# Rewriting the two attention stages of a streaming encoder: masked queries for the streams' tile, quotients on GpSimd, the causal mask as a product, the output kept in SBUF

## The reference

```python
# layer 0, prompt: causal, with a cumulative log-forget bias per head
cum = transpose(cumsum(logf, axis=1))
s = einsum('bqhd,bkhd->bhqk', q, k) * scale + cum[..., :, None] - cum[..., None, :]
s = where(key_pos <= qpos, s, -1e30)
out = einsum('bhqk,bkhd->bqhd', softmax(s), v)
# layer 0, streams: the same over 128 cached and 16 new keys of the stream itself
# layer 1, prompt: own chunk of 64 and the 8 chunks before, bias by clipped distance
s = einsum('bqhd,bkhd->bhqk', q, k) * scale + rel_bias[head, clip(dist)]
# layer 1, streams: cached and new keys of the stream, the same bias
h = h + merge_heads(out) @ w_out
```

## Time and profile before

| | |
|---|---|
| median of 3 runs | 3518.08 us (3513.18 to 3521.7) |
| the profiled execution | span 3516.8 us, 1.3 us under the median |
| stretch from 400 to 856.5 us (fox) | PE busy 347.42 us, granted clock 0.90 |
| stretch from 2168 to 2543 us (band) | PE busy 293.32 us, granted clock 0.94 |

### The profile page before, as it was taken

The page is one execution under the profiler, slowest core; times in us unless marked ns, Lnnn a source line. Parts: engine busy times, 40 slices in busy tenths (PEclk is TensorE's granted clock), DMA queues, the critical chain, the costliest instruction groups (busy, mean ns, idle before and its releaser), DMA issues. The chain is left out here.

```text
span 3516.8 us, 47851 instructions
## 1 busy us (share of the span) xinstructions
PE 3217.5 (91%) x16000; PEld 2680.0 (76%) x16000; DVE 1489.9 (42%) x2930; ACT 1174.2 (33%) x2540; POOL 423.7 (12%) x686
## 2 busy tenths in 40 slices
PE   8999577776999999999989997888699999999998
PEld 7877366665878888888878886777677888888887
DVE  3121388887243333333332221776634333333333
ACT  4232266665142211112223323777623122111122
POOL 0000245542000000000000001444300000000000
PEclk9999799998999999999999998999999999999999
DMA  4885343452441111111014884444322111111111
GB/s 153 200 250 166 137 153 141 153 178 74 125 156 60 48 36 36 36 36 52 19 51 144 241 213 160 158 157 160 106 84 78 37 51 56 36 36 36 36 36 54
DMA packets 329715, 363.82 MB, mean 103 GB/s; under 512 B 25200, under 2 KB 270976, under 8 KB 323344
## 3 DMA queue, kind: packets, MB, share of 16 engines
q1 hardware_dynamic: 329616, 362.52, 32.8%
HBM read 255.23 MB, written 120.98 MB: 107 GB/s over the span
## 5 line engine op out<-in xcount | busy, mean ns | idle before, releaser
L251 PE MATMUL ffn_gu<-ffn_gh,ffn_xh 128*128 128x512 f32 x1584 | 635.2, 401 | 0.0
L253 PE MATMUL ffn_gu<-ffn_gh,ffn_xl 128*128 128x512 f32 x1584 | 619.6, 391 | 0.0
L252 PE MATMUL ffn_gu<-ffn_gl,ffn_xh 128*128 128x512 f32 x1584 | 619.3, 391 | 0.0
L1517 DVE TENSOR_TENSOR all_h<-ffn_dn,all_h 128x1024 f32<-128x1024 f32 x198 | 242.4, 1224 | 354.3 <-PE ffn_dn L253 354.3
L1501 DVE TENSOR_TENSOR ffn_hid<-ffn_gu,ffn_gate 128x256 f32<-128x256 f32 x198 | 83.8, 423 | 722.2 <-ACT ffn_gate L1494 722.2
L1494 ACT ACTIVATE ffn_gate<-ffn_gu 128x256 f32<-128x256 f32 x198 | 75.7, 382 | 833.0 <-PE ffn_gu L253 833.0
L253 PEld LDWEIGHTS ffn_gu<-ffn_gh,ffn_xl 128*128 128x128 f32 x1584 | 298.0, 188 | 63.1
L252 PEld LDWEIGHTS ffn_gu<-ffn_gl,ffn_xh 128*128 128x128 f32 x1584 | 298.9, 189 | 56.8
L251 PEld LDWEIGHTS ffn_gu<-ffn_gh,ffn_xh 128*128 128x128 f32 x1584 | 298.4, 188 | 56.0
L251 PE MATMUL ffn_dn<-ffn_dh,ffn_hidh 128*128 128x512 f32 x792 | 308.4, 389 | 2.9 <-DVE ffn_hidl L1512 2.9
L253 PE MATMUL ffn_dn<-ffn_dh,ffn_hidl 128*128 128x512 f32 x792 | 309.0, 390 | 0.0
(11 more groups left out here) (231 smaller groups left out, 6066.2 us busy)
## 6 DMA issues: line engine op xcount, KB each, us to landing
ffn_graw<-in_w_gate_up SPq DMA_DIRECT2D x40, 1024.0 KB, 7.5
ffn_draw<-in_w_down SPq DMA_DIRECT2D x22, 1024.0 KB, 4.9
fox_ks<-k_split SPq DMA_DIRECT2D x16, 1088.0 KB, 5.6
fox_ncb<-negcum SPq DMA_DIRECT2D x16, 1088.0 KB, 10.1
band_ks<-k_split SPq DMA_DIRECT2D x16, 1088.0 KB, 5.5
qkvw_raw<-in_w_a_in SPq DMA_DIRECT2D x5, 2048.0 KB, 9.6
out<-qkvw_stage SPq DMA_DIRECT2D x36, 256.0 KB, 3.2
q_high<-qkvw_th SPq DMA_DIRECT2D x72, 128.0 KB, 2.5
```

Source lines behind the costliest of these rows:

```text
L251: pe.matmul(out, xh, wh, start=first, stop=False)
L252: pe.matmul(out, xh, wl, start=False, stop=False)
L253: return pe.matmul(out, xl, wh, start=False, stop=last)
L1517: dve.tensor_tensor(h[:, t, :], dn[:].rearrange("p a n -> p (a n)"), h[:, t, :], ALU.add).then_inc(dn_used, 1)
```

## The change

In both attention stages:

- S is scored in two blocks instead of nine. Queries of each stream are copied into a buffer that is zero elsewhere (`qmh`, `qml`, POOL), and the eight streams' products are added up in one block; the block of new keys gets its mask through a product with the identity (`idr`, `own`). Its values take 16 columns of each stream's own block.
- In fox the causal mask of the last block is added by a product of the identity with a triangle (`tri`). POOL no longer makes a bias: `ncb` is added as it is loaded, and the row's own sum, which is the same for a whole row, is left out. The gate's turning of the sums goes.
- The quotients are on POOL in both stages, and POOL also makes the upper half of the values.
- The order alternates narrow and wide tiles, S last in each head. Scores of even units lie in one PSUM bank, those of odd units in two, the turned blocks of a unit in one of two pairs of banks, the output in a bank of its own. A unit is split in one instruction on ACT and one on DVE, in step n + 5. Big groups, small groups and S have one buffer each.
- The output stays in SBUF (`att`), and the product stage splits it from there. Store and fetch go.
- At the start of a stage POOL clears the two query buffers and makes the masks (seven instructions: three memsets over 8, 8 and 2 blocks, one copy or memset and three selections of a block each), and ACT copies them to the fast format; before, POOL made the masks of S in a `pr` slot.

```diff
+    def __init__(self, ph, raw, xh, xl):
+        self.raw, self.xh, self.xl = raw, xh, xl
...
-    def fetch(self, sp, t):
-        if t >= 2:
-            sp.wait_ge(self.low_ready, t - 1)
-        sp.dma_start(self.raw[:, t % 2], self.src[:, t * P:(t + 1) * P].rearrange("(c p) n -> p c n", p=P)
-                     ).then_inc(self.loaded[t % 2], 16)
...
+        cols = slice(t * P, (t + 1) * P)
+        act.activation(self.xh[:, :, cols], self.raw[:, :, cols], ACT.Copy).then_inc(self.high_ready, 1)
...
+        return 2 if i == S else (i + 1 if fox else min(i, BAND_TILES) + 1)
...
-    by_turns = list(range(QT))
-    order = [(0, S)] + [(0, i) for i in by_turns] + [(1, by_turns[0]), (1, S)] + [(1, i) for i in by_turns[1:]]
...
+    slims, wides = (3, 2, 1, 0), (7, 6, 5, 4)
+    order = [(0, t) for two in zip(slims, wides) for t in two] + [(0, S)]
+    order += [(1, t) for two in zip(wides, slims) for t in two] + [(1, S)]
     U = len(order)
-    groups = []
-    for hh in (0, 1):
-        groups += [(hh, (S,))] + [(hh, (i, i + 1)) for i in by_turns[0::2]]
+    tiles_of = ((0, 1), (2, 3), (4, 5), (6, 7), (S,))
...
-    MAX, EXP, NORM, TURN, FIRST, OTHERS, VALUES, OUT = 1, 2, 3, 4, 4, 5, 6, 7
...
+    MAX, EXP, NORM, TURN, SPLIT, VALUES, OUT = 1, 2, 3, 4, 5, 6, 7
+    values_step = [n + VALUES for n in last_unit]
+    out_step = [n + OUT for n in last_unit]
...
+    values_at = {first + k: (hh, k) for hh, first in ((0, 0), (1, 6)) for k in range(NV)}
...
-        sp_wide = ph.ps("sp_wide", [P, 3 * WC])
-        sp_slim = ph.ps("sp_slim", [P, 2 * WC])
-        tp = ph.ps("tp", [P, TB, WC])
-        scores = [sp_wide, sp_slim]
-        op = sp_wide[:, 3 * WC - 2 * P:3 * WC]
...
+        sc = [ph.ps("sc_slim", [P, WC]), ph.ps("sc_wide", [P, 2 * WC])]
+        tp = ph.ps("tp", [P, 2, 2 * WC])
+        op = ph.ps("op", [P, WC])
...
+                        for b in range(STREAMS):
+                            sp.dma_start(sbias[hh][b * NEW:(b + 1) * NEW, 0:P],
+                                         negcum[head, (QT + b) * P:(QT + b + 1) * P].to_broadcast([NEW, P])
+                                         ).then_inc(b_loaded[hh], 16)
+                        sp.dma_start(sbias[hh][:, P:2 * P], negcum[head, (KT - 1) * P:KT * P].to_broadcast([P, P])
...
-                def store_head(p, hh):
-                    sp.wait_ge(o_done, p * G + (hh + 1) * GH)
-                    sp.dma_start(out_d[bass.ds(p * P + hh * HD, HD), :], att[hh * HD:(hh + 1) * HD, :]
-                                 ).then_inc(att_stored[hh], 16)
...
+                def normalise(p, n):
+                    w, s, m = width(order[n][1]) * P, slot_of(n), n % SMALL
+                    pool.wait_ge(inv_done, p * U + n + 1)
+                    settle(pool)
+                    pool.tensor_scalar(s[:, 0:w], s[:, 0:w], inv[:, m:m + 1], 1.0,
+                                       ALU.mult, ALU.mult).then_inc(norm_done, 1)
+                def values_high(p, n):
+                    if n in values_at:
+                        hh, k = values_at[n]
+                        k0, k1 = VSLICES[k]
+                        if (hh, k) == (0, 0):
+                            pool.wait_ge(v_loaded, (p + 1) * 16 * len(v_parts))
+                        if k == 0:
+                            wait(pool, pv_done, (p - 1) * G + (hh + 1) * GH)
+                        settle(pool)
+                        pool.tensor_copy(vs[hh][:, k0:k1, 0:HD], vraw[:, k0:k1, hh * HD:(hh + 1) * HD]
+                                         ).then_inc(vh_done, 1)
...
+                def own_queries(p, hh):
+                    pool.wait_ge(kq_loaded[hh], (p + 1) * 48)
+                    wait(pool, qk_done, p * U + (first_of_head[1] if hh else 0))
+                    for to, src in ((qmh, qh), (qml, ql)):
+                        flat = to[:].rearrange("p b q -> p (b q)")
+                        at = bass.AP(tensor=flat.tensor, offset=flat.offset,
+                                     ap=[list(flat.ap[0]), [P + NEW, STREAMS], [1, NEW]])
+                        pool.tensor_copy(at, f32(src[hh][:, S * P:TOK]).rearrange("p (b q) -> p b q", b=STREAMS)
+                                         ).then_inc(qm_done, 1)
...
+                def pair(p, last=False):
                     for n in range(U):
+                        if not fox:
+                            if n == first_of_head[1] - 4:
+                                band_bias(p, 1)
+                            if n == U - 4 and not last:
+                                band_bias(p + 1, 0)
+                        normalise(p, n)
+                        values_high(p, n)
                         values_low(p, n)
...
+                        for n, pp in stage_units(p, first, step, SPLIT):
+                            g, src, hi, _ = turned_view(n)
+                            act.wait_ge(t_done, pp * U + n + 1)
+                            wait(act, pv_done, pp * G + through_before(g))
+                            act.activation(hi, src, ACT.Copy).then_inc(th_done, 1)
...
+                        for n, pp in stage_units(p, first, step, EXP):
+                            w, s, m = width(order[n][1]) * P, slot_of(n), n % SMALL
+                            act.wait_ge(max_done, pp * U + n + 1)
+                            act.activation(s[:, 0:w], s[:, 0:w], ACT.Exp, bias=mneg[:, m:m + 1],
+                                           scale=-1.0, accum_out=rowsum[:, m:m + 1]).then_inc(exp_done, 1)
...
-                                dve.tensor_scalar(pr[s][:, 0:w], pr[s][:, 0:w], inv[:, m:m + 1], None,
-                                                  ALU.mult).then_inc(norm_done, 1)
...
+                            to = att[hh * HD:(hh + 1) * HD, bass.ds(pp, 1), tiles[0] * P:tiles[0] * P + w]
+                            dve.tensor_tensor(to.rearrange("r o n -> r (o n)"), op[0:HD, 0:w], half_out[:, 0:w],
+                                              ALU.add).then_inc(o_done, 1)
+                        for n, pp in stage_units(p, first, step, SPLIT):
+                            _, src, hi, lo = turned_view(n)
+                            dve.wait_ge(th_done, pp * U + n + 1)
+                            dve.tensor_tensor(lo, src, f32(hi), ALU.subtract).then_inc(tl_done, 1)
...
+                        pe.wait_ge(qm_done, (2 * p + hh + 1) * 2)
+                        for b in range(STREAMS):
+                            keys = slice((QT + b) * P, (QT + b + 1) * P)
+                            pe.matmul(out[:, 0:P], qmh[:, b, :], ks[hh][:, keys], start=b == 0, stop=False)
+                            pe.matmul(out[:, 0:P], qml[:, b, :], ks[hh][:, keys], start=False, stop=False)
+                        keys = slice((KT - 1) * P, KT * P)
+                        pe.matmul(out[:, P:2 * P], qh[hh][:, q], ks[hh][:, keys], start=False, stop=False)
+                        pe.matmul(out[:, P:2 * P], ql[hh][:, q], ks[hh][:, keys], start=False, stop=False)
+                        last = pe.matmul(out[:, P:2 * P], idr[:], own[:], start=False, stop=True)
+                        last.then_inc(qk_done, 1)
...
+                        if ends:
+                            last = pe.matmul(out[:, (w - 1) * P:w * P], idr[:], tri[:], start=False, stop=True)
...
+                    if tiles == (S,):
+                        for y, buf in enumerate(bufs):
+                            pe.matmul(op[:, 0:P], vs[hh][:, KT - 1, :], buf[:, P:2 * P], start=y == 0, stop=False)
+                        for b in range(STREAMS):
+                            rows = slice(b * NEW, (b + 1) * NEW)
+                            for y, buf in enumerate(bufs):
+                                last = pe.matmul(op[:, rows], vs[hh][:, QT + b, :], buf[:, rows], start=False,
+                                                 stop=b == STREAMS - 1 and y == 1)
...
+                def turn(p, n):
+                    w = width(order[n][1])
+                    pe.wait_ge(norm_done, p * U + n + 1)
+                    wait(pe, tl_done, p * U + n - 1)
+                    for b in range(w):
+                        last = pe.transpose(tp[:, n % 2, b * P:(b + 1) * P], slot_of(n)[:, b * P:(b + 1) * P], ident[:])
+                    last.then_inc(t_done, 1)
 
...
+                        for n, pp in stage_units(p, first, step, TURN):
+                            turn(pp, n)
                         for n, pp in stage_units(p, first, step, 0):
                             score(pp, n)
-                            if n in samples:
-                                scored = pp * U + n + 1
                         for g, pp in groups_at(p, first, step, values_step):
-                            values(pp, g, scored)
-                            scored = None
-                    assert scored is None
```

More of the change, by code:

```diff
@@ L484, in _ @@
                         load_x(sp, 2, NT)
-                    if turned_src is not None:
-                        for t in range(1, NT):
```

(43 more changed lines are left out.)

403 lines of the change are left out of this document (133 added, 270 removed).

## The result

The changed kernel takes 3559.43 us (median of four runs, 3544.29 to 3587.47), the kernel before 3517.47 beside it: a ratio of 1.0127, with an interval from 1.0083 to 1.0171. Forecast were 3470 and a range from 3400 to 3518.

What follows compares the result with a forecast made beforehand. PE, busy 91% of 3516.8 us, bounds the kernel except in the attention stages, where it waits for VectorE's split. Savings of 15 + 17 + 7 + 5 + 1 + 3 = 48 us give 3469, predicted as 3470, range 3400 to 3518.

Steps and rivals of the forecast that it cites:

- The ends: Starts and ends of both attention stages: hand-over 7 us, fox's beginning 5, band's first unit 1, drains 3; 16 us gained.
- VectorE, GpSimd and their covers: Per fox pair VectorE falls to about 29 us; GpSimd takes quotients and value copies, 24 us a pair, hidden.
- rival (3): Attention doesn't speed up, since freeing VectorE only moves PE's wait; only the ends remain: 3502 or 3511, chance 0.17.
- The distance of the narrow products: The streams' 16-column value matmuls start 0.11 us apart, set by loading the 128 by 128 operand.
- rival (2): Narrow matmuls start 0.065 us apart, saving 23 us: 3447; at 25 ns 43 us: 3427. Chance 0.10.
- The waits: PE waits before transposes, released by the split: 8.7 us idle a fox pair, 7.1 a band pair.
- Rival (4): Slower: return (b) runs longer, an exponential on ScalarE standing ahead of the upper half; 3534 to 3598, put at 3540, chance 0.13.
- return (b): Loop from values through upper output on ScalarE, addition and split, with single buffers: for unit 5, 2.8 us, 2.05 of it waiting.
- at the granted clock: PE work at the earlier 0.91 in fox and 0.96 in band: +1.1 us a fox pair, -0.8 a band pair.
- The sign that a pair would take as long as before: Stated sign that the forecast is wrong: a pair of heads takes as long as before, 54.6 us fox, 44.3 band.
- Fox pairs: Eight fox pairs fall from 54.6 to 52.7 us each, 1.9 a pair, 15 us in all.
- Band pairs: Eight band pairs fall from 44.3 to 42.2 us each, 2.1 a pair, 17 us in all.

Runs made afterwards that it cites:

- Experiment 3: The changed kernel with fox's quotients on VectorE again, band unchanged: 3586.8 us (ratio 1.0188).
- Experiment 6: experiment 5 plus a second output bank in both stages and two copies of band's big-group buffers: 3427.9 us (0.9737).
- experiment 2: The changed kernel with a second output bank and two copies of small-group buffers, in band of big ones too: 3489.0 us (0.9904).
- experiment 5: The changed kernel with the streams' 16-column value products made 128 columns wide, 112 of them zeros, output kept right: 3486.8 us (0.992).
- experiment 4: The changed kernel with the 16-column value products made 128 columns wide, adding other queries' products to the streams' output: 3483.2 us (0.9898).
- experiment 1: The changed kernel with 4 to 12 unread 128-column products run ahead of eight TensorE waits of a pair: 3519.8 us (1.0004).
- 7: The kernel before, with only the sixteen value products of the streams' old keys cut from 128 to 16 columns: 3514.7 us (0.9991).
- 13: The changed kernel, narrow products kept, with second output bank, two copies of band's big buffers and the split ahead of VectorE's maximum: 3412.9 us (0.9703).

## Why the prediction was wrong, step by step

**The ends were right in their sum**: 16 us forecast, 15 measured. The first fox maximum starts at 408.05 (about 407 forecast, 411.95 in the earlier trace rows). From the last addition to the first product there are 861.09 - 852.72 = 8.4 us, not 10.1; the stage change without the store costs 0.8 (1 was taken), and from the issue of the weights to the first product there are 7.5 and not 9.1. That the sum came out is partly luck. Fox's beginning gave 4.1 us (from first score to first maximum 3.3 in place of 7.3) and its last addition to the next stage's first product 5.3, together 9.3, of which only 7 arrived; band was to give 4.5 and its share of the 3 for the drains, and gave 8.

**VectorE, GpSimd and their covers were right.** VectorE is busy for 29.2 us of a fox pair (29 forecast), GpSimd for 22 (24). The copy of the values took 0.505 us for 384 columns, below my lower bound of 0.58; a quotient of that size took 0.588, so the line was right for quotients and a copy is cheaper. It was hidden either way. The groups of instructions for the turns that waited and for the copies:

```profile
L1178 PE MATMUL fox_tp<-all_ident,fox_prw 128*128 128x128 f32 x432 | 72.6, 313 | 57.3 <-DVE fox_btl L1104 55.0 <-POOL fox_prw L949 2.3
...
L961 POOL CAST fox_vs<-fox_vraw 128x384 fp32r<-128x384 f32 x32 | 16.2, 505 | 1.1 <-DMA fox_vraw<-out 1.1
```

Splits released the turns of fox's wide tiles for 55.0 us, quotients for 2.3. They bought little of TensorE's waits, though. Experiment 3 puts 10 us of VectorE back into a fox pair, and TensorE waits for 0.4 us more: the reason given for rival (3), that PE's wait for the split only moves, holds for the waits. What the move was worth came with the granted clock.

**The distance of the narrow products was right**, and with it rival (2) wrong: 0.11 us, from 2403.31 to 2403.42. The Trainium skill (TensorE: Matmul & The Clock Gate, LDWEIGHTS) gives this load by the columns of the operand alone, 128 / 1.2, an estimated 107 ns, and the trace agrees. The about 25 ns that the same page of the Trainium skill has in its section Back-to-back issue gap no run here shows.

**The waits were in their places, and too small.** Idle time of the seven pairs is 10.0 us in fox and 9.6 in band, against 8.7 and 7.1 forecast: 1.3 and 2.5 a pair too little, 30 us of the 74 by which the forecast missed the span. Rival (4) named the right place for band, the single buffers of return (b), but by an exponential that is late. In the return that ends with the first product at 2402.84 there is none: ScalarE stood idle until the values were done, and then wrote the upper half.

```profile
2401.12 0.70 ACT L1049 ACTIVATE band_bth<-band_tp 128x640 fp32r<-128x640 f32 x1 [2.45 <-PE band_op L1168]
```

That is this one return; the others are not shown. Experiment 6 puts the price of the buffers and the one bank at 4.6 us a band pair (45.1 to 40.5); experiment 2, beside narrow products, at 8.0, of which 3.0 are idle time and the rest goes with the clock.

**The step that failed is "at the granted clock".** "At the granted clock that is +1.1 us of PE a fox pair and -0.8 a band pair" took the 0.91 and 0.96 of the earlier trace rows over into the changed kernel. Measured are +1.9 and +3.8 at 0.86: 0.8 and 4.6 us a pair more than forecast, 43 us over eight pairs of each, and with the 30 of the waits that is the whole miss. A band pair was to keep TensorE busy for 35.1 us and did for 39.7; in experiment 5 it is 35.3, in experiment 4, at 0.99, 34.2. The sign that a pair would take as long as before came true for fox.

Giving the streams' value products their 128 columns back, zeros for the most part, returns 73 us and brings the kernel to 3487, 0.8% faster than before and 17 over the 3470 forecast. Even that is partly luck: a band pair is then 2.9 us over its forecast, because of the waits, and a fox pair 2.0 under it, at a clock of 0.94 that was not foreseen.

Shown are the columns (4 and 5), a part of the waits (1 and 2), and that narrow products cost next to nothing in another order (7) or with fewer waits (13). Not shown is how the two act together. That stretches of little work, waits and narrow products alike, bring the clock down is argued: the kernel before has more idle time in a fox pair (11.7 us) at 0.91, and with narrow products (7) it keeps 0.89 and 0.95. Open stay why the clock is low for 3.5 us of a band pair in one order and 14 in the other, and why fox fell to 0.82 in experiment 2.

**The sum.** Fox pairs: -15 forecast, +1.5 measured. Band pairs: -17 and +40. Ends: -16 and -15. Elsewhere: 0 and -1. Forecast -48, measured +26 in the profiled execution.

## What to carry to other kernels

Columns that are cut from products at no gain in time can still cost: here the granted clock did not carry over from one order of work to another. So read it by stretches, in the kernel before and after, and ask of each edit what TensorE is left with between two waits, not only how long that takes. A product that starts 0.11 us after the last with 16 columns or with 128 can stream zeros for nothing (experiment 5). Waits come first, though: with band's big buffers in two copies, the second output bank and the split ahead of the maximum, this change gives 3413 us, 3.0% under the kernel before, with narrow products, and 3416 with wide ones.

## What the runs showed of the hardware

- Value products of 16 and of 128 columns with a 128 by 128 operand each start 0.11 us apart alike, and the granted clock of seven band pairs was 0.86 and 0.85 with the ones (two executions) and 0.99 with the others (experiment 4).
- At the lower clock the same 16-column products start 0.21 us apart: fox's last ones in the changed kernel start at 850.67, 850.89 and 851.10.
- The clock fell in band, to 0.51 from 2427.50 to 2438.00, although no wait of the steady pair ahead of it was longer than 2.0 us.
- Filling the waits with 128-column products that nobody reads brought the kernel from 3559 to 3520 us (experiment 1).
- GpSimd copied 128 by 384 elements into fp32r in 0.505 us; the subtraction of the same size took 1.013.
